# One-core decoder trunk: three gate quads turned by VectorE and memory, table stores placed later, YP in two buffers, first transposes reordered

## What is computed

```python
def reference(x, p, ...):
    for i in range(DEPTH):
        h = _rms_norm(x, norm_mix[i])
        x = x + (_gmlp_mixer(h, ...) if i % 2 == 0 else _s5_mixer(h, ...))
        x = x + _swiglu(_rms_norm(x, norm_ffn[i]), ffn_w1[i], ffn_w3[i], ffn_w2[i])
        gate = jax.nn.sigmoid(_rms_norm(x, norm_ple[i]) @ ple_w_gate[i])
        x = x + gate * (p[i] @ ple_w_proj[i])
    return _rms_norm(x, norm_final)

def _s5_mixer(h, w_in, a_re, a_im, log_dt, b_re, b_im, c_re, c_im, d, w_out):
    u = h @ w_in                      # stage win
    ...                               # s_t = lam_bar * s_(t-1) + b_bar u_t, per group of 16 channels
    y = Re(C s) + d * u
    val, gate = jnp.split(gelu(y) @ w_out, 2, axis=-1)   # stage out1
    return val * jax.nn.sigmoid(gate)
```

## Time and profile before

| | us |
|---|---|
| median of three runs (2234.68 to 2237.42) | 2235.59 |
| the profiled execution | 2235.3 |
| its span in the profile | 2233.3 |
| TensorE matmul busy in the span | 2217.8 |
| VectorE busy | 1448.8 |
| ScalarE busy | 1024.9 |
| GpSimd busy | 493.1 |

### The profile page before, as it was taken

How to read it: one execution, slowest core, us unless ns; L and a number is a source line. 1 busy time by engine, 2 the same in 40 slices (tenths; PEclk the granted TensorE clock), 3 DMA queues, 4 the chain that set the end, 5 groups by cost and what they waited for, 6 DMA issues and landing times.

```text
span 2233.3 us, 28436 instructions
## 1 busy us (share of the span) xinstructions
PE 2217.8 (99%) x11280; PEld 1833.5 (82%) x11280; DVE 1448.8 (65%) x1612; ACT 1024.9 (46%) x1234; POOL 493.1 (22%) x470
## 2 busy tenths in 40 slices
PE   9999999999999999999999999999999999999998
PEld 7888888888888888888887788888888888888887
DVE  7879776667676666666668876555554445555666
ACT  5544444444434444445444454544444344444454
POOL 1246145456665544301003100000000000000001
PEclk9999999999999999999999999999999999999999
DMA  8668898988887898888789877777776667777774
GB/s 304 186 204 232 265 279 250 258 248 238 262 244 225 243 279 247 265 245 269 231 258 352 305 233 210 217 223 221 210 217 207 196 190 225 219 215 229 233 230 147
DMA packets 350677, 531.04 MB, mean 238 GB/s; under 512 B 106209, under 2 KB 127089, under 8 KB 349905
## 3 DMA queue, kind: packets, MB, share of 16 engines
q1 hardware_dynamic: 339456, 491.64, 73.5%
q0 software_dynamic: 8320, 30.75, 3.9%
q10 hardware_dynamic: 2768, 6.83, 0.9%
HBM read 475.67 MB, written 53.48 MB: 237 GB/s over the span
## 4 chain that ended last, share of the span: by engine, by line
PE 96%; DMA 1%; DVE 1%; issue 0%; ACT 0%; SPq 0%; ACTq 0%; DVEq 0%
PE PS L1636 62%; PE PS L1642 31%; DMA RAW<-in_s_w_out 1%; DMA X<-in_x 0%; DMA HT<-zd 0%; PE PS L1903 0%; PE PS L1904 0%; PE PS L1902 0%; PE PS L1740 0%; PE PS L1729 0%; DVE OP L1136 0%; PE PS L1667 0%; PE PS L1825 0%; DVE WLO L1110 0%; PE PS L1850 0%
## 5 line engine op out<-in xcount | busy, mean ns | idle before, releaser
L1636 PE MATMUL PS<-WHI,OP 128*128 128x512 f32 x6208 | 1537.8, 390 | 1.8 <-ACT YP L1023 1.4
L1110 DVE TENSOR_TENSOR WLO<-RAW,WHI 128x1024 fp32r<-128x1024 f32 x783 | 1020.5, 1317 | 687.8 <-ACT WHI L821 683.5
L1636 PEld LDWEIGHTS PS<-WHI,OP 128*128 128x128 f32 x6208 | 1162.3, 188 | 246.2 <-issue 3.6
L821 ACT ACTIVATE WHI<-RAW 128x1024 fp32r<-128x1024 f32 x783 | 827.5, 1062 | 999.6 <-PE PS L1642 644.7
L1642 PE MATMUL PS<-WLO,OP 128*128 128x512 f32 x3104 | 829.7, 389 | 1.3 <-DVE WLO L1110 1.3
L1642 PEld LDWEIGHTS PS<-WLO,OP 128*128 128x128 f32 x3104 | 582.5, 188 | 122.7 <-DVE WLO L1110 1.7
L805 POOL TENSOR_TENSOR ON<-X,GF 128x1024 f32<-128x1024 f32 x3 | 9.9, 3316 | 941.0 <-DVE X L1463 941.0
L706 POOL TENSOR_TENSOR TA<-BRAW,FAC 128x64 f32<-128x64 f32 x16 | 10.7, 669 | 267.4 <-DMA BRAW<-in_s_b_im 267.4
L869 ACT ACTIVATE S<-PS,RC 128x512 f32<-128x512 f32 x66 | 41.7, 684 | 37.0 <-PE PS L1642 36.9
L1136 DVE SCALAR_TENSOR_TENSOR OP<-HT,VEC,OP 128x128 fp32r<-128x128 f32 x120 | 38.2, 392 | 12.9 <-ACT OP L845 12.8
L1122 DVE TENSOR_TENSOR OP<-HT,OP 128x512 fp32r<-128x512 f32 x50 | 35.9, 760 | 15.4 <-ACT OP L836 15.4
(11 more groups left out here) (215 smaller groups left out, 956.6 us busy)
## 6 DMA issues: line engine op xcount, KB each, us to landing
RAW<-in_ffn_w SPq DMA_DIRECT2D x528, 512.0 KB, 4.3
RAW<-in_gm_w_in SPq DMA_DIRECT2D x64, 512.0 KB, 4.3
RAW<-in_s_w_out SPq DMA_DIRECT2D x64, 512.0 KB, 4.6
RAW<-in_ple_w_gate SPq DMA_DIRECT2D x56, 512.0 KB, 4.5
zd<-ZT SPq DMA_DIRECT2D x40, 512.0 KB, 3.2
HT<-zd SPq DMA_DIRECT2D x160, 128.0 KB, 5.0
RAW<-in_gm_w_out SPq DMA_DIRECT2D x32, 512.0 KB, 5.5
RAW<-in_s_w_in SPq DMA_DIRECT2D x32, 512.0 KB, 5.7
```

Source lines behind the costliest of these rows:

```text
L821: A_.activation(hi_of(t), raw_of(t), ACT.Copy).then_inc(hi_ready, 1)
L1110: V_.tensor_tensor(lo_of(t), raw_of(t), hi_of(t).bitcast(F32), ALU.subtract).then_inc(lo_ready, 1)
L1636: T_.matmul(dst[:, th, :], x_part, hi_of(t)[:, f], start=first and kk == 0 and part == 0, stop=False)
```

## The change

Six things are altered; the arithmetic is the same.

1. `gate0`'s quads 0 to 2 lose their bank and join `MOVED`; quad 3 stays with TensorE. Each is stored when the load `end + 8` has been issued (the other moved quads: 7 or 6) and fetched two loads later (the others: three). Both halves of such a quad are written per token half (`steps_of`, `tokens_of`): eight ScalarE instructions of 128x128 for four of 128x256, and eight on VectorE for four.
2. The four stores of `tabe` move from the loads `up0a + 8, 10, 12, 14` to `up0a + 20, 21, 22, 23`, behind `tabq` and `tabd` of block 0, and so behind the wait for `d_ready`.
3. GpSimd waits for `split_used` at `up0a + 12` instead of `+ 6` before it clears `EXP[1]` and builds block 0's `DT`.
4. `YP` becomes two buffers: pairs 5 and 7 use the second, in `Z`'s place (`take_y` then waits for `ut_ready` 4, the last reader of `Z`); the wait for `yg_ready` is for the last pair in the same buffer.
5. `take_y` is looked at before `y_high` at each place, and `y_high(4)` stands one place later.
6. At the start `turn(1)` goes between the two halves of tile 0, `turn(2)` and `turn(3)` after tiles 1 and 2 (before: after `turn(0)`, and both after tile 1).

```diff
@@ quads, COMES_IN, YP @@
-        last = i == len(cols) - 1 and stage in ("us", "dn0b") or stage == "gate0"
-        at = end(stage, n) + (after if last else 6 if row is None else 7)
+        last = i == len(cols) - 1 and stage in ("us", "dn0b", "gate0")
+        at = end(stage, n) + (after if last else 6 if row is None else 7 + (stage == "gate0"))
-COMES_IN = [QUADS[q][5] + 3 for q in MOVED]
+COMES_IN = [QUADS[q][5] + 3 - (QUADS[q][0] == "gate0") for q in MOVED]
+Y_HOME = [0, 0, 0, 0, 0, 1, 0, 1]
+HIGH_AT = [t + (d == DUOS - 4) for d, t in enumerate(Y_AT)]
-        YP = place("YP", [P, 2, T, 2, CH], at=s_at)
+        YP = [place(f"YP{i}", [P, 2, T, 2, CH], at=(s_at, z_at)[i]) for i in range(2)]
+        def steps_of(x_, h):
+            return x_.rearrange("p (j h i k) -> p h i k j", j=T, h=2, i=4)[:, h]
+        def tokens_of(x_):
+            return x_.rearrange("p i (k j) -> p i k j", j=T)
@@ block.sync @@
-            for i in range(4):
-                loads_to(start("up0a") + 8 + 2 * i)
-                if i == 0:
-                    sp.wait_ge(rot_ready, 1)
-                ...
                 sp.wait_ge(d_ready, b + 1)
                 sp.dma_start(tabd[b], ...).then_inc(d_out, 16)
+                if b == 0:
+                    sp.wait_ge(rot_ready, 1)
+                    for i in range(4):
+                        loads_to(BUILD_A[0] + 11 + i)
+                        ...
+                        sp.dma_start(tabe[ri, :, size * half:size * half + size], ...).then_inc(rot_out, 16)
@@ block.gpsimd @@
-                    pool.wait_ge(split_used, start("up0a") + 6)
+                    pool.wait_ge(split_used, start("up0a") + 12)
@@ block.scalar, high @@
-                            if bank is None:
+                            if bank is None and stage == "gate0":
+                                for th in range(2):
+                                    last = A_.activation(steps_of(OP[:, block_ + m, 0:TOK], th), tokens_of(HT[:, :, m, th, :]),
+                                                         ACT.Identity, scale=VEC[:, row, k:k + 1])
+                            elif bank is None:
@@ block.scalar, take_y @@
-                if d:
-                    act.wait_ge(yg_ready, d)
+                if Y_HOME[d]:
+                    act.wait_ge(ut_ready, NT)
+                earlier = [e for e in range(d) if Y_HOME[e] == Y_HOME[d]]
+                if earlier:
+                    act.wait_ge(yg_ready, earlier[-1] + 1)
@@ block.vector, low (as in high, with scalar_tensor_tensor) @@
@@ block.tensor @@
+                if between is not None:
+                    turn(between)
                 pe.wait_ge(lo_ready, t + 1)
...
-            turn(1)
             def prologue(t):
-                if t == 1:
-                    turn(2)
-                    turn(3)
+                if t in (1, 2):
+                    turn(t + 1)
```

More of the change, by code:

```diff
@@ L613, in _ @@
                 sp.dma_start(tabd[b], DT[b % 2][:, :, :, :, :].rearrange("p q r c j -> p (q r c j)")).then_inc(d_out, 16)
+                if b == 0:
+                    sp.wait_ge(rot_ready, 1)
+                    for i in range(4):
+                        loads_to(BUILD_A[0] + 11 + i)
+                        ri, half = i // 2, i % 2
+                        size = PAIRS // 2 * NC
+                        sp.dma_start(tabe[ri, :, size * half:size * half + size],
+                                     ROT[:, ri, PAIRS // 2 * half:PAIRS // 2 * (half + 1), :].rearrange("p q k -> p (q k)")
+                                     ).then_inc(rot_out, 16)
                 if b % 2:
@@ L1019, in take_y @@
                 act.wait_ge(out_of, d + 1)
[L1020 to L1021 removed]
+                if Y_HOME[d]:
[3 more added lines that the diff above has]
+                    act.wait_ge(yg_ready, earlier[-1] + 1)
                 for g in range(2):
[L1023 removed]
+                    last = A_.activation(YP[Y_HOME[d]][:, :, :, g, :].rearrange("p b i c -> p b c i"),
                                          PS[:, OUT_BANK[d] + g, 0:2 * P].rearrange("p (b c i) -> p b c i", b=2, i=T),
@@ L1044, in _ @@
                 for d in range(DUOS):
-                    if W0 + g == Y_AT[d]:
-                        y_high(d)
                     if W0 + g == OUT_AT[d] + 1:
                         take_y(d)
+                for d in range(DUOS):
+                    if W0 + g == HIGH_AT[d]:
+                        y_high(d)
                 if W0 + g == end("out1", 0):
@@ L1133, in low @@
                             b = block_ + m
-                            if bank is None:
+                            if bank is None and stage == "gate0":
+                                for th in range(2):
+                                    last = V_.scalar_tensor_tensor(
+                                        steps_of(OP[:, b, TOK:2 * TOK], th), tokens_of(HT[:, :, m, th, :]), VEC[:, row, k:k + 1],
+                                        steps_of(OP[:, b, 0:TOK].bitcast(F32), th), ALU.mult, ALU.subtract)
+                            elif bank is None:
                                 for th in range(2):
@@ L1626, in _, with tile @@
             T_ = nc.tensor
-            def tile(t, dst, block_, first, last_one):
+            def tile(t, dst, block_, first, last_one, between=None):
                 pe.wait_ge(hi_ready, t + 1)
@@ L1767, in run @@
                             pe.wait_ge(operand_ready, operands(source, k))
-                        tile(t, acc(stage, n), block_ + TK * k, j == 0, j == depth - 1)
+                        tile(t, acc(stage, n), block_ + TK * k, j == 0, j == depth - 1, between=1 if t == 0 else None)
                     hooks(t)
```

2 lines of the change are left out of this document (1 added, 1 removed).

## The result

The changed kernel takes 2242.68 us in the median (2241.41 to 2245.24, 6 runs) against 2234.87 for the kernel before (2232.42 to 2237.42, 6 runs): ratio 1.0035, interval 1.0024 to 1.0045. It is 7.8 us slower; 5.3 us faster was forecast. The profiled execution has a span of 2243.3 us against 2233.3, so 10.0 us are to be found in it.

The account below looks back on a forecast made before the run. TensorE, busy 2217.8 of 2233.3 us, was taken as the bound. Terms -2.76 (turns), -1.56 (tile 107), -1.2 (`YP`) and +0.2 (start) sum to -5.3, taking the median 2235.6 to 2230.3 us; range 2229.0 to 2233.6.

Parts of the forecast that it names:

- I take 0 for all of it: gate0: the moved quads' VectorE, ScalarE and DMA work fits in idle time and costs 0 us.
- a short pile-up is caught up: gate0: ScalarE runs up to four tiles (10.9 us) ahead and waits 1.66 us per period, so it recovers from short delays.
- the bound of 9.2: gate0: upper bound in us for ScalarE's eight strided writes, 1.154 each, against 13.5 idle.
- moved quads make `gate0` wait: Rival: ScalarE's writes and fuller memory make gate0 give back the 2.76 us, time 2233.1; chance 0.05.
- The gain of the turns: gate0 column ends: three turns leave TensorE, 0.80 + 0.12 us at each place, -2.76 us.
- The stall at tile 107: up0a: TensorE's wait on WLO goes as GpSimd no longer meets VectorE's eight instructions, -1.56 us; 0 if GpSimd is not the cause.
- Table stores: up0a: moved tabe stores cost 0; tabd goes at 325.2 and tile 120 keeps some 1.3 us of spare.
- `YP`: out1, tile 436: TensorE's wait for take_y(5) shrinks, -1.2 us (-0.2 to -1.4 depending on tile 438's load).
- Start: Kernel start: tile 0's first half ahead of turn(1) cannot begin before 8.22, +0.2 us (0 to 0.3).
- The chances: Whole prediction: forecast 0.45; rivals 0.23, 0.12, 0.07, 0.05; slower case 0.05; more than forecast 0.04.
- My 43 GB/s of added traffic: gate0: estimate for one store and one fetch of 0.5 MB per 24.5 us, just about filling the DMA share.

Follow-up runs that it names:

- f2: The changed kernel with the gate quads' fetch four loads after the store instead of two: 2244.76 us, ratio 1.0044.
- f3: The changed kernel with the gate quads' store and fetch in GpSimd's queue, two and four tiles after the column's end: 2239.88 us, ratio 1.0020.
- e1: The kernel before with only the three gate quads moved: 2244.38 us, ratio 1.0032.
- f1: The changed kernel with the three gate quads back on TensorE, all else as changed: 2233.72 us, ratio 0.9994.
- g3: The changed kernel, gate quads fetched four loads after the store into their own place, operand written behind the next column's sigmoid and residual: 2234.60 us, ratio 0.9999.
- f4: f1 plus two 512 KB memory-to-memory transfers in the places of each gate quad's store and fetch, nothing waiting for them: 2234.16 us, ratio 0.9998.
- h1: f4 with the changed kernel's SyncE and ScalarE waits put to the transfers that carry nothing: 2233.88 us, ratio 0.9993.
- i1: h1 with its two transfers per column one tile (2.72 us) later: 2233.47 us, ratio 0.9988.
- i2: h1 with its two transfers per column two tiles (5.4 us) later: 2234.11 us, ratio 0.9991.
- g2: The changed kernel storing only a sixteenth of ZT for the gate quads, every wait kept: 2234.91 us, ratio 1.0000, eleven runs from 2231.47 to 2242.77.
- i3: The changed kernel with VectorE's two transposes into ZT ahead of the next conversion in gate0: 2241.43 us, ratio 1.0022.
- g1: The changed kernel with gate0's quad 2 back on TensorE, quads 0 and 1 moved: 2238.45 us, ratio 1.0015.
- e2: The kernel before with only the tabe store places and GpSimd's wait changed: 2233.19 us, ratio 0.9986.
- e4: The kernel before with only the new order of the first transposes at the start: 2235.51 us, ratio 0.9998.
- h2: g3 with TensorE's turn of quad 3 waiting only for the operand of the last quad it turned itself: 2232.80 us, ratio 0.9991.
- h3: h2 with store and fetch in GpSimd's queue: 2231.49 us, ratio 0.9986.

## Why the prediction was wrong

**The step that failed** is "I take 0 for all of it", for what comes in the turns' place. Its reasons were idle sums: VectorE and ScalarE have the time, the memory about fills, "a short pile-up is caught up", "operands are needed only from `win` on". The sums of busy time held: VectorE's eight halves took 0.458 us each at the median for 0.392, ScalarE's eight 2.57 us together, for the bound of 9.2. But the move is a chain: sigmoid, `X`, `ZT`, store, fetch, and then the fetched data or the load behind the fetch, whichever lands last (the load in the profile after, the fetch in f2 and f3); the next sigmoid stands behind both in ScalarE's program. Its length, 28.5 us for the first round in the profile after, has to be set against the column's 24.5, and no row of busy time tells that. I priced the instructions and left out the latencies: 6.2 us from the first store's issue to its landing, 4.7 to 8.1 for the fetch, 10 for the loads behind. The prediction had the rival "moved quads make `gate0` wait", at 0.05, and capped it at the 2.76 gained; a stall that is handed from column to column has no such cap, and 12.1 us went between tiles 390 and 404.

What is shown: the quads alone make the loss (e1, f1). With same bytes and queue, writing the operand behind the sigmoid instead of ahead of it takes 10 us away (f2 against g3). That edit changes more than ScalarE's order: VectorE's half moves too, and the place `HG` frees the residual of its wait for the last operand; which of the three does it was not taken apart. Similar transfers alone, and waits that make the sigmoids up to 1.8 us late without being handed on, lose 0.7 us or nothing (f4, h1, i1, i2). A shorter link loses less, and not in every run (g2, i3).

What is argued: that the delay grows because each column hands its own to the next. The profile after reads so for two rounds of three; but the forecasts made from it missed in g1, g2, h1, i1, i2 and by little in i3, in both directions. What stays open: how much of the loss is the landing times, and how much of those is the fetch into the on-chip memory itself; f4 has no such transfer, and one into the on-chip memory that nothing waits for was not tried. Why some executions of g2 and i3 lose little is open too.

**The gain of the turns** was right: 0.80 and 0.12 us at each of the three places wherever nothing is late, 2.75 in all (g3, tile 371 to 391, -1.38 to -4.13) for 2.76. In the changed kernel 0.80 and 0.12 came at the first two as well, before the loss set in.

**The stall at tile 107**: right, 1.56 us in the trace (forecast 1.56), and GpSimd its cause as far as a move apart can show it: the eight instructions fell from 7.55 to 2.19 us. GpSimd starts at 318.10 where 316.2 was forecast, since that execution was 1.5 us behind from its start on. The rule of the Trainium skill ("SBUF — State Buffer", "Who interferes with whom") would have the stall go, and the trace agrees.

**Table stores**: 0 was right. `d_ready` was 3 us later than forecast (`tabd` 328.12 for 325.2; 1.9 of it the late start of `DT`, the rest its 10.0 us for 8.95), yet tile 120 kept 3.1 us for 1.3 forecast, TensorE being 1.5 us behind as well and the transfers shorter: between the landings of tiles 116 and 120, 12.5 us, came four loads and four stores, 1.56 us each for the 1.70 assumed.

**`YP`**: -1.2 forecast; -1.3 in its own trace and 1.0 us in the medians, neither clear of noise, for at tile 436 the traces of e2 and e4, which lack it, differ from before by -0.7 and +0.7 too. Its step, a load that takes the old wait's place, is seen. **Start**: +0.2 forecast, not to be told from nothing.

The rule of the Trainium skill that a 128x128 transpose belongs on TensorE where PSUM will do ("VectorE: DVE Perf Modes", "Rules for kernel authors") was overruled because VectorE had room. The runs agree with its outcome here, though not on VectorE's account: the moved quads lose. With the order changed (h2, h3) they gain 1.9 and 1.8 us over f1 in the traces, at tile 404, and nothing that is clear of noise in the medians.

**The chances** of the prediction add up to 1.01; nothing hangs on it.

## What to carry over

When work moves from a busy engine to idle ones through memory, add up the latencies from the event that starts it to the first thing queued behind its last step, and compare that with the period in which it recurs. If it is longer, each round starts with the last one's delay, and the queue's spare hides it just long enough to make the first rounds look free. Where it is longer, try the periodic step (here the sigmoid) ahead of the one that waits for memory, and give the fetched data a place that allows it: here this took the loss away.

## What the runs showed of the hardware

After its wait of 4.38 us TensorE ran on at the lower of its two clocks for a while. Windows of the changed kernel around tile 402 (busy time by engine, granted clock, DMA share, GB/s):

```profile
1134.00:1139.00 5.00, 0.62 (x4) 0.20 (x2) 2.21 (x4) 1.09 (x2) 0.89 (x1) 0.91 0.86 256
1139.00:1145.00 6.00, 6.00 (x15) 4.68 (x16) 3.04 (x4) 2.50 (x3) 0.00 (x0) 0.51 0.87 275
```

The granted clock is 0.51 in the second window, the lower level of 1.2 GHz; the tile took 5.28 us (1138.86 to 1144.14) for 2.72. So the 4.38 us wait cost 2.6 us more than its own length. After the 2.36 us wait before tile 399 it did not fall (the granted clock of 1125 to 1134 is 1.00, and the eight matmuls took 2.10 us); in f3 a wait of 2.64 us at the same place was followed by 3.08 us for the next eight matmuls, and in g3 one of 2.66 us by 2.09.

While a fetch of `HT` is under way, the DMA engines show a full share and move less. Three windows of the changed kernel:

```profile
1050.00:1055.00 5.00, 5.00 (x23) 4.14 (x23) 2.01 (x2) 1.13 (x2) 0.42 (x1) 1.00 1.03 381
1055.00:1060.00 5.00, 5.00 (x23) 4.13 (x23) 1.22 (x1) 1.46 (x2) 0.55 (x1) 1.00 1.10 218
1060.00:1065.00 5.00, 5.00 (x23) 4.13 (x22) 1.22 (x1) 1.00 (x2) 0.53 (x1) 1.00 1.04 365
```

218 GB/s between 381 and 365, at a share above 1 throughout; the fetch was issued from 1052.5 and landed from 1057.2 to 1061.6. In g3, which fetches later, the window 1060 to 1065 has 257 at a share of 1.08. The same half megabyte fetched to memory instead (f4) leaves 369 and 389 in the windows 1050 to 1060. My 43 GB/s of added traffic took every byte as equally dear.
